# Normalisations moved into the stage that takes their result, with pair sums on VectorE, in a three-block fp32 network on one core

## The reference: what is computed

```python
def reference(x, ...):
    x = first_block(x, ...)    # h = rmsnorm(x, norm_g); p = h @ w_in; gated linear attention,
                               # top-k sparse attention, pooling; x += y @ w_out
                               # return rmsnorm(x, final_norm_g)
    x = second_block(x, ...)   # h = _layer_norm(x) * (1 + sc1) + sh1; token mixer: z = h @ w_in;
                               # ya = silu(_layer_norm(conv(...), ln_a_g, ln_a_b)) @ w_a
                               # spatial gating of _layer_norm(v, ln_v_g, ln_v_b)
                               # x = _layer_norm(ALPHA * x + g1 * y, post1_g, post1_b)
                               # h = _layer_norm(x) * (1 + sc2) + sh2; 32 experts, top 4
                               # x = _layer_norm(ALPHA * x + g2 * y, post2_g, post2_b)
    return third_block(x, ...) # rms norm with gain and shift, then h @ w_in (state-space and
                               # linear-recurrence mixers), w_out; norm, w_up, relu^2, w_down; norm

def rmsnorm(x, g):     return x * rsqrt(mean(x * x) + EPS) * g
def _layer_norm(x, gain, bias):
    mu = mean(x); var = mean(square(x - mu))
    return (x - mu) * rsqrt(var + LN_EPS) * gain + bias
```

## Time and profile before

| | |
|---|---|
| median of 3 runs | 4418.44 us (4417.96 to 4422.14) |
| the profiled execution | 4425.26 us, its span 4423.4 us |
| TensorE busy | 3726.9 us, 84% of the span |
| VectorE, ScalarE, GpSimd busy | 1405.3, 697.6 and 231.0 us |
| TensorE's granted clock, mean | 0.894 of 2.4 GHz |

### The profile page before, as it was taken

The page is one execution under the profiler, slowest core; times in us unless marked ns, Lnnn a source line. Parts: engine busy times, 40 slices in busy tenths (PEclk is TensorE's granted clock), DMA queues, the critical chain, the costliest instruction groups (busy, mean ns, idle before and its releaser), DMA issues. The chain is left out here.

```text
span 4423.4 us, 32097 instructions
## 1 busy us (share of the span) xinstructions
PE 3726.9 (84%) x11618; PEld 1804.4 (41%) x11618; DVE 1405.3 (32%) x2445; ACT 697.6 (16%) x1294; POOL 231.0 (5%) x241
## 2 busy tenths in 40 slices
PE   7976666799979589999999998595499877889998
PEld 2524233344434234444434343343344566434444
DVE  0005522219322412111121111435825398611011
ACT  1021111101120201001010000303234233110000
POOL 0000000110000100000000000100000255000000
PEclk8985566899989789999999999697799888899999
DMA  2210732372210499999999997311222000212221
GB/s 68 81 59 32 242 125 60 106 260 76 76 48 19 198 344 401 408 400 400 408 400 409 400 407 273 115 58 49 92 74 76 24 6 1 76 59 79 72 76 38
DMA packets 219295, 729.49 MB, mean 165 GB/s; under 512 B 16207, under 2 KB 27104, under 8 KB 184374
## 3 DMA queue, kind: packets, MB, share of 16 engines
q1 hardware_dynamic: 179132, 629.94, 37.7%
q10 hardware_dynamic: 28394, 55.66, 3.6%
q0 software_dynamic: 11664, 42.47, 2.7%
HBM read 678.33 MB, written 49.69 MB: 165 GB/s over the span
## 5 line engine op out<-in xcount | busy, mean ns | idle before, releaser
L1618 PE MATMUL bank<-moe_gu,all_hT 128*128 128x512 f32 x1088 | 471.9, 594 | 0.0
L1117 PE MATMUL bank<-all_hT,early_w 128*128 128x512 f32 x896 | 389.9, 598 | 22.6 <-PEq L135 11.7
L1808 DVE TENSOR_TENSOR all_hT<-bank,moe_bias 128x512 f32<-128x512 f32 x51 | 35.3, 692 | 973.1 <-PE bank L1618 681.1
L1618 PEld LDWEIGHTS bank<-moe_gu,all_hT 128*128 128x128 f32 x1088 | 207.6, 191 | 261.1 <-issue 261.1
L1644 PE MATMUL bank<-moe_dn,moe_rows 128*128 128x512 f32 x544 | 259.8, 639 | 50.0 <-DMA moe_dn<-in_w_dn_dram 49.1
L1117 PEld LDWEIGHTS bank<-all_hT,early_w 128*128 128x128 f32 x896 | 172.0, 192 | 240.6 <-issue 240.6
L1631 PE MATMUL bank<-moe_gu,all_hT 128*64 128x512 f32 x1088 | 236.5, 592 | 1.0 <-issue 1.0
L2331 PE MATMUL bank<-all_hT,hin_w 128*128 128x512 f32 x512 | 223.4, 599 | 13.4 <-DMA hin_w<-in_w_in_dram 13.4
L1117 PE MATMUL bank<-all_hT,late_w 128*128 128x512 f32 x512 | 222.5, 598 | 10.9 <-PEq L372 10.9
L1117 PE MATMUL bank<-b_up,late_w 128*128 128x512 f32 x512 | 220.0, 592 | 2.8 <-PEq L135 2.8
L2634 PE MATMUL bank<-hg_qs,hg_ks 128*128 128x128 f32 x896 | 143.2, 313 | 87.0 <-DVE hg_ks L2580 87.0
(11 more groups left out here) (541 smaller groups left out, 4157.3 us busy)
## 6 DMA issues: line engine op xcount, KB each, us to landing
moe_gu<-in_w_gu_dram SPq DMA_DIRECT2D x136, 2048.0 KB, 21.4
moe_dn<-in_w_dn_dram SPq DMA_DIRECT2D x68, 2048.0 KB, 23.0
early_w<-in_w_in_dram SPq DMA_DIRECT2D x13, 2048.0 KB, 9.1
expert_rows<-conv_zeros POOLq DMA_DIRECT2D x49, 512.0 KB, 17.2
early_w<-in_w_mod_dram SPq DMA_DIRECT2D x12, 2048.0 KB, 8.1
early_w<-in_ada_w_dram SPq DMA_DIRECT2D x12, 2048.0 KB, 7.9
hin_w<-in_w_in_dram SPq DMA_DIRECT2D x10, 2048.0 KB, 8.4
late_w<-in_w_up_dram SPq DMA_DIRECT2D x8, 2048.0 KB, 9.0
```

Of the source, the lines that this page charges most:

```text
L1117: mm = nc.tensor.matmul(B[b][:], w[:, k, m * P:(m + 1) * P], src[:, i * KT + k if stacked else k, :], start=(k == 0), stop=(k == KT - 1))
L1618: mm = nc.tensor.matmul(B[bank][:], xb2[:, k, :], gu[:, q, kk, col:col + HALF], start=(k == 0), stop=(k == KT - 1))
L1808: after(vec.tensor_tensor(g, gate[:], bias[0], ALU.add), 1)
```

## The change

`norm` becomes a class `Norm`, whose parts (`sums` for TensorE, `vector`, `scalar`, `clear` for GpSimd) can be put at the head of the same engine's part in another stage. A function `norm` that wraps one `Norm` in a block of its own remains, and n5 and n12 still use it.

- n1 goes into `projection`; n4 into the `linear` "wa"; n11 into the `linear` "up".
- n2 and n3 go into `mixer_in` together, n6 and n7 into `route` (which takes over the loads of n6's stage), n8 and n9 into `ssd_inputs`. The second of such a pair gets `ready=`, the first: its work on tile k waits only for the first's tile k. `finish_modulation`, and for n8 also `lower_bounds`, now stand ahead of the pair.
- The stage's first product waits for the normalised tile k just ahead of the matmul that takes it (`normed[-1].wait(pe, k)`).
- In each sum of squares tiles 4 and 5, and 6 and 7, are added by VectorE first, so TensorE has 6 matmuls in place of 8. In each sum for a mean it has 5 in place of 8 (tiles 0 and 1 alone, then pairs), or 6 with `ready` (tiles 0 to 3 alone).
- n9, which has `ready` and no mean, has its squares made by VectorE in place of ScalarE.
- Scratch space moves: n1 uses `y_rest` and `dq`, n11 the last eight tiles of `up`, and n6's `rstd` is the buffer `part` of `route`.

```diff
+class Norm:
+    def __init__(self, core, ctx, name, src, dst, ones, scratch, gain, bias=None, centre=False, func=None, eps=EPS,
+                 ready=None, rstd=None):
...
+        self.alone = 2 if ready is None else 4
...
+    def sums(self, pe):
+        nc, ones = self.core.nc, self.ones
+        mean_ps, square_ps = self.core.bank[0], self.core.bank[1]
+        if self.centre:
+            for k in range(self.alone):
+                if self.ready is not None:
+                    pe.wait_ge(self.ready.done, k + 1)
+                nc.tensor.matmul(mean_ps[:], ones[:], self.src[:, k, :], start=(k == 0), stop=False)
+            for i, k in enumerate(range(self.alone, KT, 2)):
+                pe.wait_ge(self.paired, i + 1)
+                mm = nc.tensor.matmul(mean_ps[:], ones[:], self.scratch(k), start=False, stop=(k == KT - 2))
+            mm.then_inc(self.summed, 1)
+        for k in range(4):
+            pe.wait_ge(self.squared, k + 1)
+            nc.tensor.matmul(square_ps[:], ones[:], self.scratch(k), start=(k == 0), stop=False)
+        for i, k in enumerate((4, 6)):
+            pe.wait_ge(self.square_paired, i + 1)
+            mm = nc.tensor.matmul(square_ps[:], ones[:], self.scratch(k), start=False, stop=(k == 6))
+        mm.then_inc(self.square_summed, 1)
+
+    def vector(self, dve):
+        nc, scratch = self.core.nc, self.scratch
+        if self.centre:
+            for k in range(self.alone, KT, 2):
+                if self.ready is not None:
+                    dve.wait_ge(self.ready.done, k + 2)
+                nc.vector.tensor_tensor(scratch(k), self.src[:, k, :], self.src[:, k + 1, :],
+                                        ALU.add).then_inc(self.paired, 1)
+            dve.wait_ge(self.summed, 1)
...
+        elif self.ready is not None:
+            for k in range(KT):
+                dve.wait_ge(self.ready.done, k + 1)
+                nc.vector.tensor_tensor(scratch(k), self.src[:, k, :], self.src[:, k, :],
+                                        ALU.mult).then_inc(self.squared, 1)
+        for k in (4, 6):
+            dve.wait_ge(self.squared, k + 2)
+            nc.vector.tensor_tensor(scratch(k), scratch(k), scratch(k + 1), ALU.add).then_inc(self.square_paired, 1)
+        dve.wait_ge(self.std_ready, 1)
+        nc.vector.reciprocal(self.rstd[:], self.rstd[:]).then_inc(self.inv_ready, 1)
...
-def linear(core, stream, name, passes, src, evict, stacked=False, more=None, background=None):
+def linear(core, stream, name, passes, src, evict, stacked=False, more=None, background=None, normed=()):
...
         @block.tensor
         def _(pe):
+            for n in normed:
+                n.sums(pe)
             for i in range(passes):
...
                         for k in range(KT):
+                            if normed and i + b == 0:
+                                normed[-1].wait(pe, k)
                             mm = nc.tensor.matmul(B[b][:], w[:, k, m * P:(m + 1) * P],
...
-        norm(core, "n3", xT, hT, ones, tile(0), mod[:, 8:16], mod[:, 0:8], centre=True, eps=LN_EPS)
...
+            n2 = Norm(core, s, "n2", xT, xT, ones, tile(0), core.columns("final_norm_g"))
+            n3 = Norm(core, s, "n3", xT, hT, ones, tile(0), mod[:, 8:16], mod[:, 0:8], centre=True, eps=LN_EPS, ready=n2)
+            mixer_in(core, hT, c["b_in"], c["conv_w"], c["conv_b"], z, conv, a["y_dram"], (n2, n3))
...
+                        n8 = Norm(core, n, "n8", xT, xT, ones, y_hg, core.columns("post2_g_2"), core.columns("post2_b_2"),
+                                  centre=True, eps=LN_EPS)
+                        n9 = Norm(core, n, "n9", xT, hT, ones, y_hg, c["gain1"], mod[:, 0:8], ready=n8)
+                        ssd_inputs(core, si, hT, w_in, c["conv_w"], c["conv_b"], zs, xbc, dt_raw, (n8, n9))
```

More of the change, by code:

```diff
@@ L368, in norm @@
+def norm(core, name, src, dst, ones, scratch, gain, **more):
     nc = core.nc
-    plain = func is None and bias is None
-    func = func or ACT.Identity
-    mean_ps, square_ps = core.bank[0], core.bank[1]
     with ExitStack() as ctx:
[L373 to L376, removed]
+        alone = Norm(core, ctx, name, src, dst, ones, scratch, gain, **more)
@@ L377, in norm @@
         block = ctx.enter_context(nc.Block())
[L378 to L383, removed]
         @block.gpsimd
         def _(pool):
-            nc.gpsimd.memset(eps_col[:], eps).then_inc(eps_set, 1)
+            alone.clear(pool)
         @block.tensor
         def _(pe):
[L391 to L398, removed]
+            alone.sums(pe)
@@ L410, in _ @@
[L410 to L417, removed]
+            alone.vector(dve)
@@ L430, in _ @@
[L430 to L434, removed]
+            alone.scalar(act)
 OFF = {}
@@ L1066, in first_block @@
         mix_out(core, xT, y_gla, y_dsa, y_pool)
-        with ExitStack() as s:
-            (scratch,) = bufs(nc, s, "b1f", scratch=[P, KT, T])
-            norm(core, "n2", xT, xT, ones, scratch, fg)
 CONV_W, SGU_G = 31, 8
@@ L1325, in second_block, with route @@
     experts(core, a, xT, hT, ident, ones, mod, c)
-def route(core, spare, hT, ident, ones, gate, loaded, rows_dram, row, weight, share, unit_expert, n_steps):
+def route(core, spare, hT, ident, ones, gate, loaded, rows_dram, row, weight, share, unit_expert, n_steps,
+          normed, loads):
     nc = core.nc
@@ L1352, in route, with _ @@
         block = ctx.enter_context(nc.Block())
+        @block.sync
+        def _(sp):
+            loads(sp)
         @block.gpsimd
         def _(pool):
+            for n in normed:
+                n.clear(pool)
             pool.wait_ge(copied, 8)
@@ L2899, in third_block @@
             (up,) = bufs(nc, s, "b3", up=[P, 32, T])
-            norm(core, "n11", xT, hT, ones, up[:, 0:KT, :], c["gain2"], mod[:, 24:32])
             (squared,) = sems(nc, s, "up_squared")
@@ L2909, in square @@
                     nc.vector.tensor_tensor(up[:, n, :], up[:, n, :], up[:, n, :], ALU.mult).then_inc(squared, 1)
-            linear(core, late, "up", 4, hT, ("scalar", emit), more=square)
+            with ExitStack() as n:
+                n11 = Norm(core, n, "n11", xT, hT, ones, up[:, 3 * KT:, :], c["gain2"], mod[:, 24:32])
+                linear(core, late, "up", 4, hT, ("scalar", emit), more=square, normed=(n11,))
             linear(core, late, "down", 4, up, add_gated(40), stacked=True)
```

160 lines of the change are left out of this document (112 added, 48 removed).

## The result

| | before | changed kernel |
|---|---|---|
| median | 4418.2 us (4411.7 to 4422.1, 4 runs) | 4358.0 us (4351.2 to 4360.9, 4 runs) |
| ratio | | 0.9861, 95% interval 0.9846 to 0.9877 |
| the profiled execution's span | 4423.4 us | 4358.0 us |
| TensorE busy, mean granted clock | 3726.9 us, 0.894 | 3703.0 us, 0.895 |

The change makes the kernel 61.4 us faster (54 to 68). The forecast was 71 us, a median of 4347.5 in a range from 4337 to 4357. The measured median lies 1.0 us above the upper end of that range (the ratio on the 4418.4 us that the forecast started from gives 4357.0), and the gain is 86% of the one forecast.

A forecast was written before the change was run, and what follows sets the result against it. The prediction took chains of latencies through the normalisations, where TensorE waits for the stage before, as the bound. Site gains sum to 71.0 us; 4425.3 becomes 4354.3, less 6.8 for the median: 4347.5 us, range 4337 to 4357.

The forecast's parts named there:

- The sum over the sites: Gains added over the normalisations n1 to n9, n11 and n12: 71.0 us.
- the clearing: Border where semaphores are cleared, ahead of `mixer_in`, comes somewhere else: +0.75 us, booked under n2 and n3.
- Sums: Fewer TensorE tiles: 2.55 us less per mean, 1.7 per plain sum of squares, 1.15 per sum after centring.
- Tails: Next stage's first product needs only tile 0: TensorE's idle falls from 10.94 to 5.6 us, plain norm 9.85 to 4.9.
- Pairs: Second norm's sum starts tile by tile at n2/n3, n6/n7, n8/n9: 7.8 (net 7.0), 6.25 and 5.5 us less.
- The unknown costs: Clock at shorter idles, VectorE beside GpSimd, waits per tile, borders with clearing; slow first tiles kept, nothing taken for GpSimd.
- rival 1: At first tiles behind merged norms the clock stays up over shorter idles: 13.0 us less, 4334 us; chance 0.05.
- rival 2: Around n2 and n3 VectorE is held by GpSimd's zeroing issues: 9 us lost, 4356.5 us; chance 0.06.
- rival 3: Next product's matmuls don't start before the last tile, so tails don't overlap: 30 us back, 4377.5 us; chance 0.04.
- rival 4: Zeroing gets in front of the weights for `mixer_in`'s first product: +71 us, 4419 us or more; chance 0.02.
- The step that failed: From sum to median: profiled 4425.3 less 71.0 gives 4354.3, moved by 6.8 us to a median of 4347.5.

The follow-up runs named there:

- filled: The changed kernel plus unread TensorE matmuls of ones behind the sum of squares of each merged normalisation: 4340.4 us, ratio 0.9811 to the kernel before.
- last_tile: The changed kernel, but the next stage's products wait for all eight normalised tiles: 4382.0 us, ratio 0.9913 to the kernel before.
- before2: The kernel before, unchanged, profiled a second time: 4423.0 us in that execution.
- again: The changed kernel, unaltered, timed a second time: 4354.2 us, ratio 0.9851 to the kernel before.
- no_pairs: The changed kernel with merged stages kept, but TensorE sums all eight tiles itself: 4382.4 us, ratio 0.9902 to the kernel before.
- zero_late: The changed kernel with GpSimd's zeroing held back until n3's last tile is written: 4341.1 us in one execution.
- zero_timed: The same kernel as "zero_late" (zeroing held until n3's last tile), this time timed: 4358.3 us, ratio 0.9856 to the kernel before.
- pairs_only: The kernel before with only VectorE's pair sums added, all normalisations staying stages of their own: 4390.7 us, ratio 0.9923 to the kernel before.
- whole_first: The changed kernel, but the second normalisation of a pair waits for all of the first: 4367.8 us, ratio 0.9855 to the kernel before.

## Why the prediction was right, and where not

**The sum over the sites.** 70.7 us against 71.0, in one pair of traces. n4 is off by 1.15, of which 0.8 is the clearing that the forecast had under n2 and n3; no other site is off by more than 0.8. That the sum comes so close is partly luck, since the errors below have both signs. Term by term:

- *Sums.* The mean's gain at n4 is 2.58 (7.11 to 4.53; forecast 2.55), the squares' after centring 1.03 (7.13 to 6.10; forecast 1.15). n1's gained 2.6 (9.56 to 6.94) in place of 1.7, since in this execution the slow start was shorter: its first four tiles took 5.23 us, n2's of the same form 6.09. That is n1's 7.4 in place of 6.65.
- *Tails.* TensorE's idle became 5.83 (forecast 5.6) and 5.04 (4.9). The waits per tile cost nothing that shows, and the products of the five dense stages weren't held (the router's was, as forecast: 5.89 us in place of 3.64).
- *Pairs.* n3's mean sum ended 9.1 us after n2's first output, not 8.4, since four tiles were slow where I had taken three (6.53 us against 6.0). In n7 it was 8.9 against 8.5. For n9's four tiles I had 5.95; they took 5.91, and the whole stretch 12.47 against 12.65. `mixer_in` began at 845.06, forecast 843; its own site gained 15.7 (15.2 forecast: without the clearing, and with 0.6 saved ahead of it, it made up for the late sum), and the missing 2 us were lost ahead of it, between n1 and n2, where the text is the same.

**The unknown costs.** The clock (rival 1): the first tiles run slow as before, 47.59 against 48.75 us, so the slow start was rightly kept in the sum. "filled" shows what rival 1 would have been worth: 11.9 us at the first tiles (13.0 in the prediction), 18 in all. VectorE beside GpSimd (rival 2, whose 9 us would have given 4356.5, near the first median): refuted by the rows, 742 to 751 ns for outputs beside the issues and away from them, the reciprocal 3.35 us, an addition 0.68. GpSimd's issues didn't take longer either (median 2011 ns, before 2013). The rule of the Trainium skill ("SBUF — State Buffer", Who interferes with whom) that the prediction set against the change is for GpSimd instructions that read SBUF. The prediction took DMA issues for such, which that section doesn't say: it says of `tensor_tensor` that a probe found it not to stall DMA. The trace agrees with that, with additions of 0.68 us and issues of 2011 ns beside each other. Tails that don't overlap (rival 3): "last_tile" builds it and costs 27.8 us (30 in the prediction), while in the change the idle is 5.83 us. Zeroing ahead of the weights (rival 4): the first product was released by ScalarE's tile (5.83 us, `all_hT` L466), not by a DMA.

**The step that failed** is the last one, from the sum to the median. I took 4425.3 - 71.0 and moved it by the 6.8 us between one profiled execution and the median of three, as if all that lies outside the sites were a constant (4418.4 - 71.0 comes to the same). It isn't. Span less sites (and less what only moved), in the order of the runs:

| | span | less sites | less moved | rest |
|---|---|---|---|---|
| before, before2 | 4423.4, 4421.2 | 282.2, 283.0 | none | 4141.1, 4138.2 |
| change, again | 4358.0, 4347.7 | 204.0, 204.0 | 5.4 | 4148.6, 4138.2 |
| no_pairs, last_tile | 4381.0, 4378.5 | 231.6, 233.9 | 5.4 | 4144.0, 4139.2 |
| zero_late, zero_timed | 4339.3, 4352.1 | 204.6, 207.5 | 5.4 | 4129.3, 4139.2 |
| pairs_only, whole_first | 4402.1, 4379.2 | 249.9, 215.3 | none, 5.4 | 4152.1, 4158.5 |

The rest runs from 4129 to 4159 us. Its mean is 4139.7 in the two executions of the kernel before and 4142.4 in the seven of merged kernels; of these 2.7 us the accounts above explain 2.2 (2.0 of the router's product and 0.8 of clearing, less 0.6). Most of the spread is the recurrence: without it the rest is 3837.9 and 3831.2 before, and 3831.2 to 3843.1 in the merged kernels, with a mean of 3836.3. So these profiles show no loss outside the sites that isn't accounted for, but each single one can be 6 us off or more, which a single profile can't foresee. The sites of "zero_timed" vary too, 3.5 us more than in "again"; 1.6 of them are at n11 (shown in the last section).

The timings give 61.4, 65.9 and 63.7 us (the last from "zero_timed"), 5 to 9 us below the 70.7 of the sites. The intervals reach 68.0, 72.5 and 71.2, so 71 isn't excluded by the last two, but three values lie on one side. Whether some 5 us are really lost outside the sites, or the three timings came out low by chance, stays open: no place was found for such a loss. What makes the recurrence take 298 to 316 us is open as well, beyond the wait named above.

That rival 2's 4356.5 us was nearer to the first median than the forecast is chance: the rows show none of its waits.

## What to carry to other kernels

Where a chain of small operations goes from engine to engine, the end of a stage costs little by itself (0.2 to 0.9 us here); the cost is that the consumer waits for the last tile, and letting it start with the first brought 28 us of 66. Moving late tiles of a sum to another engine pays as far as that engine is free when they arrive: about 1.7 us a sum of squares when VectorE was free (1.65 at n12), 1.0 when it was still centring, 0.6 for n3's mean, where it was still writing n2's outputs. And an idle of 5 us ahead of TensorE costs twice, once as idle and once as a slow first tile: cheap idle matmuls in it were worth another 18 us, more than any one stage's merging brought. Once they are in place, another engine may be the next bound, as VectorE was at n3. Judge such differences by medians beside the kernel before: single runs of "whole_first" lay up to 19 us off their own median here.

## What was not expected of the hardware

TensorE's granted clock falls after shorter idles than the 5.20 us of the earlier trace rows, and not always. In the timeline at n11, the same code, after the same 1.98 us of idle, in the changed kernel and then in "zero_timed":

```profile
3873.84 3.70 PE L410 MATMUL bank<-b_up,all_ones 128*128 128x512 f32 x8 [1.98 <-ACT b_up L459]
```

```profile
3865.27 5.40 PE L410 MATMUL bank<-b_up,all_ones 128*128 128x512 f32 x8 [1.98 <-ACT b_up L459]
```

Four tiles took 3.70 us in one execution and 5.40 in the other, at a granted clock of 1.00 and 0.68. The kernel before had such pairs too, in its expert loop: at 1961.53, after an idle of 3.42 us, the next 3 us were granted 0.50; at 2382.24, after 3.46 us, they were granted 1.00. After the idles of 5.04 and 5.83 us ahead of the products the start was slow at all five places of the changed kernel (granted clock 0.71 to 0.77 over the first tile).
